# A fused mLSTM and sliding-window attention trunk: x loaded in one row, gate weights on ScalarE's DMA queue, the input gate scaled on ScalarE, two weight units multiplied by their gain beside the gate scans

## The chip, the core and the metric

The kernel runs on one core of a Trainium2 chip. Its time is device microseconds from launch to end. An engine is named here as in the trace: PE (matrix products), DVE (vector), ACT (scalar, table functions), POOL (GpSimd), SP (issues DMAs). SPq and ACTq are the DMA-issuing instructions on SP and on ACT; they run in the order of that engine's program.

## What is computed

One mLSTM layer with its SwiGLU, a shared K/V projection, one sliding-window attention layer with its SwiGLU, a final RMSNorm; x is 1024 x 1024, all in float32. The change lies in the first stage: the norm of x, the gates, and what the first head needs from them.

```python
def rmsnorm(x, g):
    return (x * lax.rsqrt(jnp.mean(x * x, axis=-1, keepdims=True) + EPS)) * g

def mlstm_mixer(x, w_in, b_gates, head_norm, w_out):      # x: rmsnorm of the input with a_norm
    proj = x @ w_in
    q, k, v, o, gates = jnp.split(proj, [QK_W, 2 * QK_W, 2 * QK_W + V_W, 2 * QK_W + 2 * V_W], axis=-1)
    gates = GATE_CAP * jnp.tanh((gates + b_gates) / GATE_CAP)      # GATE_CAP = 15
    ig, fg = jnp.split(gates, 2, axis=-1)                          # 4 heads each
    lf = jax.nn.log_sigmoid(fg)
    h = mlstm_chunkwise(q * DQK_A ** -0.5, k, v, ig, lf)           # running sums of lf, running maxima with ig
    h = h * lax.rsqrt(jnp.mean(h * h, axis=-1, keepdims=True) + EPS) * head_norm
    return (h.reshape(Bsz, S, V_W) * jax.nn.sigmoid(o)) @ w_out
```

## The kernel before

Every float32 product is made of three passes of split operands: a tile is copied rounded (`write_hi`, ACT) and the rest is subtracted (`write_lo`, mostly DVE). Weights of the first layer come in units of 128 columns: unit 0 holds the gate weights (`U_GATES`), units 1 to 6 the six column blocks of head 0 (`U_HEADS + 0` to `+ 5`). A unit is loaded into one of three `raw` buffers by SP, multiplied in place by the norm's gain on POOL (`gain`, L952), rounded into `w_split` by ACT (L1190) and subtracted by DVE (L1596; the unit `U_HEADS + 3` by POOL, L1094). Only then is its raw buffer free for the unit three later, for which SP waits.

The order is written out by hand, engine by engine; semaphores count the steps. The first stage is this.

- SP loads x in eight tiles of 128 rows (L647). After three of them it issues two loads of the gate weights (L658, L659: 1024 runs of 16 bytes each) and the gain (L650: 1024 runs of 4 bytes), then the other five tiles, then units 1 and 2.
- For each tile ACT squares and sums (L1195), DVE forms the mean (L1601), POOL takes the power -0.5 (L940), DVE scales the tile (`x_normed`, L1607), PE transposes it (L2137), ACT rounds the transpose (L1201) and DVE subtracts (L1614). POOL multiplies the gate unit by its gain between the fourth and the fifth power; ACT and DVE split the gate unit at tile 5.
- PE multiplies the gate unit with all of x in two halves (L2103, L2105), then units 1 and 2. Beside these two units runs the gate chain on ACT and DVE: tanh of both gates (L1401, L1403), the input gate times 15 on DVE (L1836), exp (L1408), 1 + exp (L1838), ln (L1410), a correction (L1841), exp (L1413), product (L1845), log forget (L1847), the two scans (L1850 a sum, L1852 a maximum), differences (L1855 to L1864) and three last exponentials (L1416, L1418, L1419).
- PE then waits for ACT's L1418 (`gate_act` at least 5) and transposes the stacked gate rows (L2333); next come the v products (L2320 to L2324) and at last the chunk products of head 0 (L2369 on). POOL stores two gate rows and loads them spread over the partitions (L1098, L1103), SP waits for the end of the gate chain before it loads the first rows of `w_out`.
- `gate_dve` counts the DVE steps of the gate chain, `gate_act` those of ACT. POOL multiplies units 4, 5 and 6 by the gain as they arrive, without looking at these counts.

Of the kernel before, what the change touches and what calls it, by code (L numbers as in the profile page):

```python
# [151 lines left out]
def yoco_kernel(nc, x, a_norm, a_w_in, a_b_gates, a_head_norm, a_w_out, kv_norm, w_kv, b_kv,  # L152
# [169 lines left out]
    with ExitStack() as ctx:  # L322
# [301 lines left out]
        def _(sp):  # L624
# [21 lines left out]
            def load_x(t):  # L646
                sp.dma_start(X[:, t, :], x2[t * P:(t + 1) * P, :]).then_inc(x_loaded[t], 16)  # L647

            def load_gains(i, g):
                sp.dma_start(gcol[:, i, :], g.rearrange("(k p) -> p k", p=P), allow_slow_non_contiguous=True  # L650
                             ).then_inc(a_gain_loaded if i == 0 else gains_loaded, 16)

            for t in range(3):
                load_x(t)
            sp.wait_ge(gate_w_cleared, 1)
            gates = raw[:, 0, :].rearrange("p (k n) -> p k n", k=KT)
            g0 = 2 * NH_A * DQK + 2 * D
            sp.dma_start(gates[:, :, 0:NH_A], win[:, :, g0:g0 + NH_A]).then_inc(gate_w_loaded, 16)  # L658
            sp.dma_start(gates[:, :, 32:32 + NH_A], win[:, :, g0 + NH_A:g0 + 2 * NH_A]).then_inc(gate_w_loaded, 16)  # L659
            load_gains(0, a_norm[0, :])  # L660
            for t in range(3, TT):
                load_x(t)
# [39 lines left out]
            sp.wait_ge(gate_dve, 12)  # L702
            sp.wait_ge(gate_act, 7)
# [213 lines left out]
        def _(pool):  # L917
# [169 lines left out]
            for j in range(3, 6):  # L1087
                gain(Unit(U_HEADS + j))
# [21 lines left out]
            pool.wait_ge(gate_dve, 10)  # L1110
# [3 lines left out]
            pool.wait_ge(gate_act, 7)  # L1114
# [64 lines left out]
        def _(act):  # L1179
# [201 lines left out]

            K = uses.stage(NORM)
            for t in range(TT + 2):
                if t < TT:
                    act.wait_ge(x_loaded[t], 16)
                    square(0, t)
                if t >= 2:
                    xt_hi(K, t - 2)
                if t == 5:
                    write_hi(Unit(U_GATES))  # L1390
                if t >= TT:
                    write_hi(Unit(U_HEADS + t - TT))
# [16 lines left out]
            act.wait_ge(gate_dve, 3)  # L1409
# [4 lines left out]
            write_hi(Unit(U_HEADS + 3))  # L1414
            act.wait_ge(gate_dve, 8)
            act.activation(G[32:32 + NH_A, :], mrow[:], ACT.Exp, scale=-1.0).then_inc(gate_act, 1)  # L1416
            act.wait_ge(gate_dve, 12)
# [170 lines left out]
        def _(dve):  # L1588
# [227 lines left out]
            for t in range(TT + 2):  # L1816
                if t < TT:
                    mean_square(0, t)
                if t >= 2:
                    xt_lo(0, K, t - 2)  # L1820
                if t < TT:
                    x_normed(0, t)
                if t == 5:
                    write_lo(Unit(U_GATES))
            for j in range(2):
# [8 lines left out]
            K = uses.stage(BANK_45)  # L1834
            dve.wait_ge(bank_free[5], K[5] + 1)
            dve.tensor_scalar(ig[:], ig[:], GATE_CAP, None, ALU.mult).then_inc(gate_dve, 1)  # L1836
# [3 lines left out]
            dve.wait_ge(gate_dve, 3)  # L1840
            dve.scalar_tensor_tensor(enf[:], one_enf[:], -1.0, enf[:], ALU.add, ALU.subtract  # L1841
                                     ).then_inc(gate_dve, 1)
            dve.wait_ge(gate_dve, 4)
            dve.wait_ge(gate_act, 3)
            dve.tensor_tensor(enf[:], enf[:], fg[:], ALU.mult).then_inc(gate_dve, 1)  # L1845
            dve.wait_ge(gate_dve, 5)
            dve.tensor_tensor(lf[:], enf[:], lnu[:], ALU.subtract).then_inc(gate_dve, 1)  # L1847
            dve.wait_ge(gate_dve, 6)
            dve.wait_ge(const_step, 11)
            dve.tensor_tensor_scan(brow[:], chunk_mask[:], lf[:], 0.0, ALU.mult, ALU.add  # L1850
                                   ).then_inc(gate_dve, 1)
            dve.tensor_tensor_scan(mrow[:], lf[:], ig[:], 0.0, ALU.add, ALU.max  # L1852
                                   ).then_inc(gate_dve, 1)
            dve.wait_ge(gate_dve, 8)
# [4 lines left out]
            dve.wait_ge(gate_dve, 11)  # L1859
# [229 lines left out]
        def _(pe):  # L2089
# [209 lines left out]
            def head(h, turn, first):  # L2299
# [227 lines left out]
```

## Time and profile before

| | us |
|---|---|
| three runs: median (lowest, highest) | 2083.46 (2080.19, 2085.99) |
| the profiled execution, its own time | 2087.04 |
| its span in the trace | 2085.4 |
| PE busy in the span | 2020.8 (97%) |
| DVE, ACT, POOL busy | 1352.5, 925.8, 1211.7 |

The profiled execution is 3.6 us above the median of the three runs, and its span is 1.6 us shorter than its own time. Busy time of PE is modelled from pipelined matmuls, so 97% says where its waits are few, not that it runs at its peak. The whole change lies before 60 us of the span; what it moves later is only what starts earlier or later by it.

### The profile page before, as it was taken

The page shows a single profiled execution, that of the slowest core. Times are in us where ns is not written, and L with a number is a line of the kernel's source. Part 1 is how long each engine was busy: PE and PEld are TensorE (multiplying, and loading weights), DVE is VectorE, ACT ScalarE, POOL GpSimd, SP SyncE. Part 2 cuts the span into 40 slices and gives each one's busy share as a digit, 9 for nine tenths or more (in the row PEclk, how much of TensorE's full clock was granted, in tenths as well). Part 3 has the DMA queues.
Part 4 walks back from the last instruction along what each step waited for, and adds up shares of the span by engine and source line. Part 5 has one row for each costly group of instructions (what it writes and reads, how often), then busy time and mean ns, then how long its engine had stood idle before and what let it go on. Part 6 is the DMA issues. An engine that isn't in the chain of part 4 may idle for free.

```text
span 2085.4 us, 29248 instructions
## 1 busy us (share of the span) xinstructions
PE 2020.8 (97%) x9992; PEld 1660.8 (80%) x9992; DVE 1352.5 (65%) x1929; ACT 925.8 (44%) x1951; POOL 1211.7 (58%) x1058
## 2 busy tenths in 40 slices
PE   7999999899999999999999999899999999999998
PEld 6888988678888888888878666578788888888886
DVE  7663642568777767554665677768776676645566
ACT  6444343255555545422344454536544554532233
POOL 5531521464889988655664111264888788756565
PEclk9999999999999999999999999999999999999999
DMA  5655535843777787695844100564567666687673
GB/s 153 200 203 180 176 141 201 292 139 119 229 256 246 239 265 244 238 390 177 268 138 81 31 21 21 202 212 122 184 231 250 224 234 230 213 329 286 216 266 114
DMA packets 295431, 415.03 MB, mean 199 GB/s; under 512 B 40040, under 2 KB 218232, under 8 KB 295296
## 3 DMA queue, kind: packets, MB, share of 16 engines
q1 hardware_dynamic: 260752, 307.87, 45.0%
q10 hardware_dynamic: 33120, 100.68, 13.4%
q0 software_dynamic: 1424, 4.77, 0.8%
q8 instruction: 74, 1.21, 0.2%
q14 instruction: 61, 0.50, 0.1%
HBM read 259.09 MB, written 154.17 MB: 198 GB/s over the span
## 4 chain that ended last, share of the span: by engine, by line
PE 84%; DVE 7%; issue 3%; DMA 2%; ACT 2%; POOL 2%; SPq 0%; ACTq 0%; DVEq 0%; POOLq 0%
PE ps L2200 21%; PE ps L2202 20%; PE ps L2201 20%; PE ps L2103 8%; PE ps L2105 4%; PE ps L2464 1%; PE ps L2323 1%; PE ps L2324 1%; PE ps L2320 1%; PE ps L2493 1%; DVE mats L1643 1%; DMA scratch_y<-y_head 1%; PE ps L2483 1%; DVE forms L1741 1%; PE ps L2255 1%
## 5 line engine op out<-in xcount | busy, mean ns | idle before, releaser
L2200 PE MATMUL ps<-forms,mats 128*128 128x512 f32 x2016 | 790.7, 392 | 22.9 <-DVE X L1666 11.8
L2202 PE MATMUL ps<-forms,mats 128*128 128x512 f32 x2016 | 786.6, 390 | 0.0
L2201 PE MATMUL ps<-forms,mats 128*128 128x512 f32 x2016 | 786.2, 390 | 0.0
L1000 POOL TENSOR_TENSOR mats<-sum_a,mats 128x256 fp32r<-128x256 f32 (+2 forms) x384 | 405.8, 1062 | 373.2 <-ACT mats L1234 372.1
L2200 PEld LDWEIGHTS ps<-forms,mats 128*128 128x128 f32 x2016 | 379.6, 188 | 111.0 <-issue 19.6
L2202 PEld LDWEIGHTS ps<-forms,mats 128*128 128x128 f32 x2016 | 379.4, 188 | 79.9
L2201 PEld LDWEIGHTS ps<-forms,mats 128*128 128x128 f32 x2016 | 379.7, 188 | 77.4
L1666 DVE TENSOR_TENSOR X<-ps,X 128x512 f32<-128x512 f32 x390 | 267.6, 690 | 204.3 <-PE ps L2202 202.2
L1234 ACT ACTIVATE mats<-sum_a 128x256 fp32r<-128x256 f32 (+2 forms) x392 | 201.1, 516 | 336.6 <-PE ps L2202 317.0
L1643 DVE TENSOR_TENSOR mats<-stream_raw,mats 128x256 fp32r<-128x256 f32 (+2 forms) x302 | 279.0, 925 | 43.8 <-ACT mats L1234 43.1
L1234 ACT ACTIVATE mats<-stream_raw 128x256 fp32r<-128x256 f32 (+2 forms) x302 | 156.5, 520 | 250.8 <-PE ps L2202 237.0
L1622 DVE TENSOR_TENSOR prep_forms<-prep_raw,prep_forms 128x512 fp32r<-128x512 f32 x115 | 155.5, 1352 | 66.6 <-ACT prep_forms L1213 65.7
L986 POOL TENSOR_TENSOR sum_a<-stream_raw 128x256 f32<-128x256 f32 (+2 forms) x96 | 108.9, 1134 | 144.1 <-DVE mats L1643 55.9
L2103 PE MATMUL ps<-xT_hi,w_split 128*128 128x512 f32 x416 | 174.6, 420 | 0.0
L2103 PE MATMUL ps<-xT_lo,w_split 128*128 128x512 f32 x416 | 162.6, 391 | 0.0
L2105 PE MATMUL ps<-xT_hi,w_split 128*128 128x512 f32 x416 | 130.3, 391 | 0.0
L987 POOL TENSOR_TENSOR sum_a<-stream_raw 128x256 f32<-128x256 f32 (+2 forms) x96 | 121.3, 1264 | 0.0
L991 POOL TENSOR_TENSOR sum_a<-sum_a,stream_raw 128x256 f32<-128x256 f32 (+2 forms) x96 | 115.0, 1198 | 0.0
L995 POOL TENSOR_TENSOR sum_a<-stream_raw,sum_a 128x256 f32<-128x256 f32 (+2 forms) x96 | 109.5, 1140 | 6.9
L2103 PEld LDWEIGHTS ps<-xT_hi,w_split 128*128 128x128 f32 x416 | 78.2, 188 | 28.7 <-issue 13.9
L952 POOL TENSOR_TENSOR raw<-raw,gain_cols 128x1024 f32<-128x1024 f32 x34 | 73.2, 2163 | 39.4 <-DMA raw<-in_a_w_in_dram 21.9
L2105 PEld LDWEIGHTS ps<-xT_hi,w_split 128*128 128x128 f32 x416 | 78.1, 188 | 17.0
(230 smaller groups left out, 2705.7 us busy)
## 6 DMA issues: line engine op xcount, KB each, us to landing
forms<-scratch_forms ACTq DMA_DIRECT2D x182, 512.0 KB, 5.2
scratch_forms<-prep_forms SPq DMA_DIRECT2D x161, 512.0 KB, 3.4
stream_raw<-in_w_gate_up_dram SPq DMA_DIRECT2D x88, 512.0 KB, 5.4
scratch_forms<-head_forms SPq DMA_DIRECT2D x49, 512.0 KB, 2.6
scratch_hidden<-hidden SPq DMA_DIRECT2D x84, 256.0 KB, 5.4
prep_raw<-in_w_down_dram SPq DMA_DIRECT2D x38, 512.0 KB, 5.7
stream_raw<-scratch_hidden SPq DMA_DIRECT2D x32, 512.0 KB, 4.4
forms<-scratch_forms SPq DMA_DIRECT2D x28, 512.0 KB, 8.0
```

Source lines behind the costliest of these rows:

```text
L987: pool.tensor_tensor(s[2], a11, a21, ALU.subtract)
L991: pool.tensor_tensor(s[1], s[0], a11, ALU.subtract).then_inc(ssum, 2)
L1000: pool.tensor_tensor(blocks(m[:, q, 1, :], it.width), stream_source(it, q), blocks(m[:, q, 0, :].bitcast(F32), it.width), ALU.subtract).th ...
L1234: act.activation(blocks(mats[w][:, q, 0, :], w), stream_source(it, q), ACT.Copy).then_inc(hi_s, 4 if it.plain and q == 3 else 1)
L1622: dve.tensor_tensor(dst[:, 1, :], split_source(prep_raw[j % 2], prep_t, q), dst[:, 0, :].bitcast(F32), ALU.subtract).then_inc(prep_lo, 1)
L1643: dve.tensor_tensor(blocks(m[:, q, 1, :], it.width), stream_source(it, q), blocks(m[:, q, 0, :].bitcast(F32), it.width), ALU.subtract).the ...
L1666: dve.tensor_tensor(xv, ps[:, s + BANK_OF[q], :], before, ALU.add).then_inc(d_add, 1)
L2103: ms_ = [mm(ps[:, b + half, :], ah, t[:, c[half]], start=start and t is bh, stop=False) for half in halves for t in (bh, bl)]
L2105: ms_ += [mm(ps[:, b + half, :], al, bh[:, c[half]], start=False, stop=stop) for half in halves]
L2200: mm(dst, ah, bh, start=OPENS[q] and k == 0, stop=False, skip_group_check=True)
L2201: mm(dst, ah, bl, start=False, stop=False, skip_group_check=True)
L2202: m = mm(dst, al, bh, start=False, stop=k == w - 1, skip_group_check=True)
```

## The change

SP issues the eight tiles of x without anything between. The three loads of gate weights and gain go to ACT's queue; they stand ahead of ACT's first activation. The gate unit is split at tile 4 instead of 5. The input gate is scaled on ACT, after the third exponential, and the DVE step is gone; `U_HEADS + 3` is rounded by ACT ahead of the ln instead of after the exponential. POOL multiplies unit `U_HEADS + 3` where it did, but `U_HEADS + 4` and `+ 5` only after `gate_dve` has reached 5, which is the end of log forget. The counts that others wait for are shifted to match.

```diff
-            for t in range(3):
-                load_x(t)
-            sp.wait_ge(gate_w_cleared, 1)
-            gates = raw[:, 0, :].rearrange("p (k n) -> p k n", k=KT)
-            g0 = 2 * NH_A * DQK + 2 * D
-            sp.dma_start(gates[:, :, 0:NH_A], win[:, :, g0:g0 + NH_A]).then_inc(gate_w_loaded, 16)
-            sp.dma_start(gates[:, :, 32:32 + NH_A], win[:, :, g0 + NH_A:g0 + 2 * NH_A]).then_inc(gate_w_loaded, 16)
-            load_gains(0, a_norm[0, :])
-            for t in range(3, TT):
+            for t in range(TT):
                 load_x(t)
...
-            sp.wait_ge(gate_dve, 12)
-            sp.wait_ge(gate_act, 7)
+            sp.wait_ge(gate_dve, 11)
+            sp.wait_ge(gate_act, 8)
             load_head_row(0)
...
-            for j in range(3, 6):
-                gain(Unit(U_HEADS + j))
+            gain(Unit(U_HEADS + 3))
...
-            pool.wait_ge(gate_dve, 10)
+            pool.wait_ge(gate_dve, 5)
+            for j in range(4, 6):
+                gain(Unit(U_HEADS + j))
+            pool.wait_ge(gate_dve, 9)
             pool.dma_start(scr_negm, negm[:]).then_inc(negm_stored, 16)
...
+            act.wait_ge(gate_w_cleared, 1)
+            gates = raw[:, 0, :].rearrange("p (k n) -> p k n", k=KT)
+            g0 = 2 * NH_A * DQK + 2 * D
+            act.dma_start(gates[:, :, 0:NH_A], win[:, :, g0:g0 + NH_A]).then_inc(gate_w_loaded, 16)
+            act.dma_start(gates[:, :, 32:32 + NH_A], win[:, :, g0 + NH_A:g0 + 2 * NH_A]).then_inc(gate_w_loaded, 16)
+            act.dma_start(gcol[:, 0, :], a_norm[0, :].rearrange("(k p) -> p k", p=P), allow_slow_non_contiguous=True
+                          ).then_inc(a_gain_loaded, 16)
             K = uses.stage(NORM)
...
-                if t == 5:
+                if t == 4:
                     write_hi(Unit(U_GATES))
...
             act.activation(enf[:], fg[:], ACT.Exp, scale=-GATE_CAP).then_inc(gate_act, 1)
-            act.wait_ge(gate_dve, 3)
+            write_hi(Unit(U_HEADS + 3))
+            act.wait_ge(gate_dve, 2)
             act.activation(lnu[:], one_enf[:], ACT.Ln).then_inc(gate_act, 1)
             act.wait_ge(gate_act, 2)
 
             act.activation(fg[:], lnu[:], ACT.Exp, scale=-1.0).then_inc(gate_act, 1)
-            write_hi(Unit(U_HEADS + 3))
-            act.wait_ge(gate_dve, 8)
+            act.activation(ig[:], ig[:], ACT.Copy, scale=GATE_CAP).then_inc(gate_act, 1)
+            act.wait_ge(gate_dve, 7)
...
-                if t == 5:
+                if t == 4:
                     write_lo(Unit(U_GATES))
...
-            K = uses.stage(BANK_45)
-            dve.wait_ge(bank_free[5], K[5] + 1)
-            dve.tensor_scalar(ig[:], ig[:], GATE_CAP, None, ALU.mult).then_inc(gate_dve, 1)
+            uses.stage(BANK_45)
...
+            dve.wait_ge(gate_act, 4)
             dve.tensor_tensor_scan(mrow[:], lf[:], ig[:], 0.0, ALU.add, ALU.max
                                    ).then_inc(gate_dve, 1)
...
-                    pe.wait_ge(gate_act, 5)
+                    pe.wait_ge(gate_act, 6)
```

ACT's program from its start, before: the table load and the first squares stand first.

```order
L1195 ACT_TABLE_LOAD
L1195 ACTIVATE squares,ssq<-X 128x1024 x3
L1201 ACTIVATE xT_hi<-ps 128x4x128 x2
L1195 ACTIVATE squares,ssq<-X 128x1024
L1201 ACTIVATE xT_hi<-ps 128x4x128 x2
```

And now, with three DMAs ahead of the table load.

```order
L1379 DMA raw<-in_a_w_in_dram 128x8x4
L1380 DMA raw<-in_a_w_in_dram 128x8x4
L1381 DMA gain_cols<-in_a_norm_dram 128x8x1
L1189 ACT_TABLE_LOAD
L1189 ACTIVATE squares,ssq<-X 128x1024 x3
```

What moved: nothing in ACT's program can start before the three issues are through.

ACT's program in the gate chain, before (`w_split<-raw` is a `write_hi`).

```order
L1408 ACTIVATE exp_neg_f<-gate_f 4x1024
L1410 ACT_TABLE_LOAD
L1410 ACTIVATE ln_one_plus<-one_plus_exp 4x1024
L1413 ACT_TABLE_LOAD
L1413 ACTIVATE gate_f<-ln_one_plus 4x1024
L1190 ACTIVATE w_split<-raw 128x1024
L1416 ACTIVATE gate_stack<-m_row 4x1024
```

And now.

```order
L1409 ACTIVATE exp_neg_f<-gate_f 4x1024
L1184 ACTIVATE w_split<-raw 128x1024
L1412 ACT_TABLE_LOAD
L1412 ACTIVATE ln_one_plus<-one_plus_exp 4x1024
L1415 ACT_TABLE_LOAD
L1415 ACTIVATE gate_f<-ln_one_plus 4x1024
L1416 ACTIVATE gate_i<-gate_i 4x1024
L1418 ACTIVATE gate_stack<-m_row 4x1024
```

What moved: the rounding of unit 4 now stands ahead of the first table load of the chain, and the scaling of the input gate is new.

POOL's program between the norm and the first gate row that it stores, before (`raw<-raw,gain_cols` is a `gain`).

```order
L1085 MEMSET chunk_mask 4x8
L952 TENSOR_TENSOR raw<-raw,gain_cols 128x1024 x3
L1094 TENSOR_TENSOR w_split<-raw,w_split 128x1024
L1111 DMA scratch_neg_m<-neg_M 4x1024
L1098 DMA SwT<-scratch_neg_m 128x1024
```

And now.

```order
L1077 MEMSET chunk_mask 4x8
L944 TENSOR_TENSOR raw<-raw,gain_cols 128x1024
L1085 TENSOR_TENSOR w_split<-raw,w_split 128x1024
L944 TENSOR_TENSOR raw<-raw,gain_cols 128x1024 x2
L1105 DMA scratch_neg_m<-neg_M 4x1024
L1089 DMA SwT<-scratch_neg_m 128x1024
```

What moved: two of the three multiplications stand behind the subtraction of unit 4, and the diff makes them wait for log forget.

## Rows read from the trace of the kernel before

**Rows 1.** The page's head.
```profile
span 2085.4 us, 29248 instructions
```
**Rows 2.** Timeline, PE: start, length, instruction, idle time before it and its releaser.
```profile
15.62 3.89 PE L2137 MATMUL ps<-ident,x_normed 128*128 128x128 f32 x16 [3.06 <-DVE x_normed L1607]
...
21.28 0.57 PE L2103 MATMUL ps<-xT_hi,w_split 128*128 128x512 f32 x1
...
58.85 1.84 PE L2333 MATMUL ps<-ident,gate_stack 128*128 128x128 f32 x8 [2.66 <-ACT gate_stack L1418]
...
90.82 0.67 PE L2369 MATMUL ps<-v_one,SwT 128*128 128x257 f32 x2 [2.24 <-ACT v_one L1455]
```
**Rows 3.** The chain that ended last, in order of time: start, length, what.
```profile
60.78 5.47 DMA scratch_decay<-m_prev
...
86.95 2.60 DMA scratch_forms<-head_forms
```
**Rows 4.** Timeline, SP's DMA issues: start, time to issue.
```profile
2.32 0.43 SPq L658 DMA_DIRECT2D raw<-in_a_w_in_dram  x1
2.80 0.90 SPq L659 DMA_DIRECT2D raw<-in_a_w_in_dram  x1
3.74 3.40 SPq L650 DMA_DIRECT2D gain_cols<-in_a_norm_dram  x1
7.18 2.68 SPq L647 DMA_DIRECT2D X<-in_x_dram  x5
```
**Rows 5.** DMA issues by line: count, KB each, median us from issue to landing.
```profile
raw<-in_a_w_in_dram SPq DMA_DIRECT2D x2, 16.0 KB, 5.5
```
**Rows 6.** Stretches: length, PE busy (instructions), granted clock, DMA share, GB/s.
```profile
5.00:6.00 1.00, 0.00 (x0) 1.00 1.00 397
...
8.00:9.00 1.00, 1.00 (x7) 1.00 1.08 53
...
17.00:18.00 1.00, 1.00 (x5) 0.50 1.20 290
...
60.00:64.00 4.00, 4.00 (x27) 0.69 0.94 300
```
**Rows 7.** Timeline, ACT, the first stage.
```profile
0.94 1.28 ACT L1195 ACT_TABLE_LOAD   x1 [0.94 <-PEq L2516]
4.54 1.06 ACT L1195 ACTIVATE squares<-X 128x1024 f32<-128x1024 f32 x1 [2.32 <-DMA X<-in_x_dram]
...
11.18 1.06 ACT L1195 ACTIVATE squares<-X 128x1024 f32<-128x1024 f32 x1 [1.16 <-DMA X<-in_x_dram]
```
**Rows 8.** Timeline, DVE, the gate chain.
```profile
35.87 1.99 DVE L1836 TENSOR_SCALAR gate_i<-gate_i 4x1024 f32<-4x1024 f32 x1 [0.31 <-ACT gate_f L1403]
37.79 2.38 DVE L1838 TENSOR_SCALAR one_plus_exp<-exp_neg_f 4x1024 f32<-4x1024 f32 x1
40.20 2.80 DVE L1841 SCALAR_TENSOR_TENSOR exp_neg_f<-one_plus_exp,exp_neg_f 4x1024 f32<-4x1024 f32 x1
43.74 1.21 DVE L1845 TENSOR_TENSOR exp_neg_f<-exp_neg_f,gate_f 4x1024 f32<-4x1024 f32 x1 [0.74 <-ACT gate_f L1413]
44.99 3.30 DVE L1847 TENSOR_TENSOR log_forget<-exp_neg_f,ln_one_plus 4x1024 f32<-4x1024 f32 x1
48.33 2.28 DVE L1850 TENSOR_TENSOR_SCAN b_row<-chunk_mask,log_forget 4x1024 f32<-4x1024 f32 x1
```
**Rows 9.** Timeline, POOL.
```profile
0.93 0.95 POOL L918 MEMSET raw<- 128x1024 f32 x1 [0.29 <-POOLq L2516]
...
13.12 1.89 POOL L952 TENSOR_TENSOR raw<-raw,gain_cols 128x1024 f32<-128x1024 f32 x1
...
34.44 5.18 POOL L952 TENSOR_TENSOR raw<-raw,gain_cols 128x1024 f32<-128x1024 f32 x2 [3.02 <-DMA raw<-in_a_w_in_dram]
39.90 2.03 POOL L952 TENSOR_TENSOR raw<-raw,gain_cols 128x1024 f32<-128x1024 f32 x1 [0.27 <-DMA raw<-in_a_w_in_dram]
44.67 2.55 POOL L1094 TENSOR_TENSOR w_split<-raw,w_split 128x1024 fp32r<-128x1024 f32 x1 [2.73 <-ACT w_split L1190]
```

More of the change, by code:

```diff
@@ L650, in load_gains @@
                 sp.dma_start(gcol[:, i, :], g.rearrange("(k p) -> p k", p=P), allow_slow_non_contiguous=True
-                             ).then_inc(a_gain_loaded if i == 0 else gains_loaded, 16)
-            for t in range(3):
-                load_x(t)
-            sp.wait_ge(gate_w_cleared, 1)
-            gates = raw[:, 0, :].rearrange("p (k n) -> p k n", k=KT)
-            g0 = 2 * NH_A * DQK + 2 * D
-            sp.dma_start(gates[:, :, 0:NH_A], win[:, :, g0:g0 + NH_A]).then_inc(gate_w_loaded, 16)
-            sp.dma_start(gates[:, :, 32:32 + NH_A], win[:, :, g0 + NH_A:g0 + 2 * NH_A]).then_inc(gate_w_loaded, 16)
-            load_gains(0, a_norm[0, :])
-            for t in range(3, TT):
+                             ).then_inc(gains_loaded, 16)
+            for t in range(TT):
                 load_x(t)
@@ L1113, in _ @@
             load_neg_row(0)
-            pool.wait_ge(gate_act, 7)
+            pool.wait_ge(gate_act, 8)
             pool.dma_start(scr_einter, einter[:]).then_inc(rows_stored, 16)
@@ L1413, in _ @@
             act.activation(fg[:], lnu[:], ACT.Exp, scale=-1.0).then_inc(gate_act, 1)
-            write_hi(Unit(U_HEADS + 3))
-            act.wait_ge(gate_dve, 8)
+            act.activation(ig[:], ig[:], ACT.Copy, scale=GATE_CAP).then_inc(gate_act, 1)
+            act.wait_ge(gate_dve, 7)
             act.activation(G[32:32 + NH_A, :], mrow[:], ACT.Exp, scale=-1.0).then_inc(gate_act, 1)
-            act.wait_ge(gate_dve, 12)
+            act.wait_ge(gate_dve, 11)
             act.activation(G[64:64 + NH_A, :], brow[:], ACT.Exp).then_inc(gate_act, 1)
@@ L1833, in _ @@
             write_lo(Unit(U_HEADS + 2))
-            K = uses.stage(BANK_45)
-            dve.wait_ge(bank_free[5], K[5] + 1)
-            dve.tensor_scalar(ig[:], ig[:], GATE_CAP, None, ALU.mult).then_inc(gate_dve, 1)
+            uses.stage(BANK_45)
             dve.wait_ge(gate_act, 1)
             dve.tensor_scalar(one_enf[:], enf[:], 1.0, None, ALU.add).then_inc(gate_dve, 1)
-            dve.wait_ge(gate_dve, 3)
+            dve.wait_ge(gate_dve, 2)
             dve.scalar_tensor_tensor(enf[:], one_enf[:], -1.0, enf[:], ALU.add, ALU.subtract
                                      ).then_inc(gate_dve, 1)
-            dve.wait_ge(gate_dve, 4)
+            dve.wait_ge(gate_dve, 3)
             dve.wait_ge(gate_act, 3)
             dve.tensor_tensor(enf[:], enf[:], fg[:], ALU.mult).then_inc(gate_dve, 1)
+            dve.wait_ge(gate_dve, 4)
+            dve.tensor_tensor(lf[:], enf[:], lnu[:], ALU.subtract).then_inc(gate_dve, 1)
             dve.wait_ge(gate_dve, 5)
-            dve.tensor_tensor(lf[:], enf[:], lnu[:], ALU.subtract).then_inc(gate_dve, 1)
-            dve.wait_ge(gate_dve, 6)
             dve.wait_ge(const_step, 11)
@@ L1851, in _ @@
                                    ).then_inc(gate_dve, 1)
+            dve.wait_ge(gate_act, 4)
             dve.tensor_tensor_scan(mrow[:], lf[:], ig[:], 0.0, ALU.add, ALU.max
                                    ).then_inc(gate_dve, 1)
-            dve.wait_ge(gate_dve, 8)
+            dve.wait_ge(gate_dve, 7)
             dve.tensor_tensor(G[0:NH_A, :], ig[:], brow[:], ALU.subtract).then_inc(gate_dve, 1)
@@ L1858, in _ @@
             dve.tensor_copy(mprev[:, 0, 1:TT], chunks(mrow)[:, 0:TT - 1, P - 1]).then_inc(gate_dve, 1)
-            dve.wait_ge(gate_dve, 11)
+            dve.wait_ge(gate_dve, 10)
             last_negm = chunks(negm)[:, :, P - 1:P]
```

## The prediction, made before the changed kernel ran

> **What bounds the kernel now.** I read the page's head first, then PE's waits, then the chain of waits, since only a stretch in which PE waits, or runs at the lower clock, can give time back. The span is 2085.4 us [rows 1]; the change touches its first 60. PE waits there three times for something the change moves [rows 2]: 3.06 us before the transposes at 15.62, after which the granted clock stands at 0.50, the lower of its two levels (1.2 GHz) [rows 6]; 2.66 us at 58.85, for ACT's exponential of the gate rows, after which the clock means 0.69 over 60 to 64; and 2.24 us at 90.82, before the first chunk product. Between them PE runs without a gap, from the first gate product at 21.28 to 56.19 (58.85 less 2.66).
>
> The chain that ended last does not leave the gate work at 58.85 [rows 3]: it goes from the last exponentials over POOL's stored gate rows (the transfer of 5.47 us from 60.78), the sums and forms of the first `w_out` rows, to a store at 86.95 and so to 90.82. So what decides until 90.82 is the gate chain, not PE: a gate chain that ends d earlier brings the end forward by d, until PE itself is late. PE has 2.66 us of wait and about 1.3 us of slow clock to give at 58.85 ((1 - 0.69) x 4 us), and 2.24 us at 90.82, some 6 us together. A later gate chain is paid in full.
>
> So two sums are wanted: when the gate products of PE end (A), and how long the gate chain lasts from there (B).
>
> **A. The loads and the norm.** Before, the five last tiles of x are issued from 7.18 on, because three small transfers stand ahead; the third alone takes 3.40 us to issue [rows 4]. Their 3072 short runs also cost the DMA engines time: 53 GB/s from 8 to 9 us at a share of 1.08, where whole tiles give 397 [rows 6]. With x in one row, a tile takes 0.512 MB / 397 GB/s = 1.3 us, and tile 3 lands near 9 us instead of 11.18. ACT was done with the tiles before it at 10.02 (11.18 less its wait of 1.16 [rows 7]), so tile 3 starts 1.2 us earlier at best. From there ACT, DVE and PE are near their own pace (about 2 us a tile on ACT), and PE's transposes and the gain multiplication (1.89 us on POOL [rows 9], which holds DVE back) take part of it again. Splitting the gate unit at tile 4 puts its 1.06 us on ACT and 1.2 us on DVE before tile 5 instead of behind it: it makes the weights ready sooner, but the gate products wait for the transposes of tile 5, which come later by it. Following each engine's order, I get the gate products 0.7 us earlier. If the clock keeps its upper level (2.4 GHz), eight transposes take about 1.0 instead of 1.95 us (3.89 for sixteen [rows 2]), and the gain is 2.5 at most.
>
> Against it stands ACT's queue. Its three issues start at 1.9 us, when POOL has cleared the buffer [rows 9], and hold the table load (1.28 us [rows 7]) and the first square. With 0.43, 0.90 and again 0.43 us [rows 4] ACT is free at 1.9 + 1.76 + 1.28 = 4.9, 0.4 us behind the 4.54 of before, and that is absorbed where tile 2 is waited for. With 3.40 for the third it is 7.9, and A loses about 2 us instead of winning 0.7. I take the short issues: ACT's queue is empty at that moment, while SP's held three tiles.
>
> The larger unknown is when the small transfers land beside x. Alone behind three tiles the weights landed 5.5 us after issue [rows 5]. POOL takes up the gate unit after the fourth power, near 12 us, and the fifth power is queued behind it; DVE's fifth scaling, PE's fifth transposes and ACT's rounding wait for that. Landing by 12 costs nothing. If each DMA engine takes one run from either queue in turn, its 192 short runs go with 64 rows of 4 KB of x (0.16 us each: 10.5 us in all), and the rest beside the 512-byte runs of units 1 and 2; the gain then lands near 19 or 20 us. The gate multiplication moves from 13.12 to about 20 and A loses 7. The bounds of A are +2.5 and -8; I take +0.7.
>
> On how two queues share an engine the profile says nothing for such small runs. The Trainium skill (DMA: Bandwidth & Descriptors, section Queues, rings and completion order) has each engine go round the queues by packets of typically 9 to 17 descriptors; by that 192 short ones would be gone after 12 to 20 turns, and A stays at its small gain. No row here shows it.
>
> **B. The gate chain.** From both tanh at 35.87 to PE's transposes at 58.85 it lasts 23 us. Its DVE steps are stretched wherever POOL works. The 1 + exp from 37.79 ends at 40.17, 0.55 us after POOL's pair of multiplications ends at 39.62; the correction from 40.20 ends at 43.00, 1.07 after POOL's next ends at 41.93; log forget from 44.99 ends at 48.29, 1.07 after POOL's subtraction ends at 47.22 [rows 8, 9]. The product at 43.74, with POOL idle, takes 1.21. So DVE stands still until POOL is through.
>
> Now, on the old clock: exp ends at 36.93 (1.06 us, as any ACT pass over 1024 elements [rows 7]); 1 + exp no longer stands behind the input gate's 1.99 us, only behind the gain of unit 4, which ends near 37.0, and is done near 37.75; the correction is done near 39.0. ACT rounds unit 4 until 38.0, loads its table until 39.3, ln until 40.35, table until 41.65, exp until 42.7: 0.9 us before the old chain, whose product, waiting for it, started at 43.74 and so now starts at 42.8. Here the moved rounding is on the path, because the table load used to run while ln waited; it costs its 1.05 us and ln still starts 0.9 earlier. POOL's subtraction of unit 4 now lies beside the correction and ends near 41, so log forget takes 1.21 like the product and ends at 45.25 instead of 48.29. Gain so far: 3.0 us. The input gate on ACT (1.06 us until 43.8) is hidden: the second scan wants it at 47.5 (45.25 + 2.28).
>
> Then two multiplications come due at the very moment the first scan starts. No row of before has a scan beside POOL, so their price lies between 0 and 2 x 1.89 = 3.8 us. The nearest rows are the correction and log forget, which like the scan read two operands and were held to the full; I take 3.8. B then is 3.0 - 3.8 = 0.8 us longer. POOL has nothing else to do before it stores the first gate row, which comes after both scans, so POOL's own delay is free.
>
> The Trainium skill (SBUF, State Buffer, section Who interferes with whom) says that a vector instruction with two inputs in SBUF and a GpSimd instruction that reads SBUF exclude each other for their whole length. The rows of the correction and of log forget agree to a tenth of a us; by this rule moving work beside the scans only moves the stall, by the opposite assumption B gains all 3.0.
>
> **The sum.** A gives 0.7, B takes 0.8: +0.1 us on the profiled 2087.04 us, whose span is 2085.4. The profiled execution is 3.6 us above the median of 2083.46, so the forecast against that median is 2083.5.
>
> **The rivals.**
> 1. The scans are not held. B gains 3.0 and A 0.7: 2083.5 - 3.7 = 2079.8. For it: a scan takes 2.28 us for 1024 elements where the product takes 1.21, so it reads at about half the rate and may leave room. Against it: all three stretched steps above. If PE then waits over 3 us at 90.82, its clock can drop as it did after 3.06 and 2.66 us; up to 1.3 of the gain goes again.
> 2. The gate weights land late (slower). In turn with x, as worked out: A loses 7 and B 0.8, so 2083.5 + 7.8 = 2091.3. It decides from a landing after about 12 us and is paid one for one. For it: the short runs filled the DMA engines (share 1.08 at 53 GB/s) even alone. Against it: 4 us head start over the place where they are needed.
> 3. ACT is held at its third issue for the 3.40 us that SP was: A loses 2, B 0.8: 2086.3. For it: the same transfer behind the same two. Against it: no tiles of x in that queue.
>
> **Chances.** Forecast 0.37, rival 1 0.23, rival 2 0.25, rival 3 0.15. A change below 0.3% (6.2 us) is about what a measurement can't tell from none. The largest gain, 2.5 + 3.0, stays under it; only with an error of the runs does it pass: faster 0.08. Slower by more needs rival 2 with held scans: 0.19. The same 0.73. The forecast's own range is 2081 to 2086; with the rivals 2078 to 2091.5.
>
> **What will show it.** Squares of tile 3 start near 10 us; first square near 4.9 (7.9 under rival 3); the gate unit's multiplication near 12 (near 20 under rival 2); first gate product near 20.6; log forget takes 1.2 us; the scans and the step behind them together last 3.8 us longer than 2 x 2.28 + 1.21, or each its old length under rival 1; PE's wait at the gate transposes grows by 0.8 or vanishes, and in that case the wait before the first chunk product grows. I am wrong if the time falls by more than 6 us, or if a later stage, in which no instruction is changed, has its own new wait.

## The result: 12 us slower, outside the forecast range

| | before | after |
|---|---|---|
| median | 2083.46 us (7 runs) | 2095.64 us (7 runs) |
| profiled execution | 2087.04 us | 2100.39 us |
| its span | 2085.4 us | 2098.8 us |

The ratio after to before is 1.0057, with a 95% interval of 1.0039 to 1.0074; it leaves out one disturbed run of after (2882 us), and without that run after lies between 2090.95 and 2100.39 us. The forecast was 2083.5 us and its range ended at 2091.5. The change costs 12.2 us by the medians and 13.4 by the spans of the two profiled executions.

### The profile page after: what moved, and what is told of

It reads as the page before. It is cut to its first block, busy times and chain, and to the rows that moved or that the text cites. A ratio compares the mean times of both kernels' runs of the same rounds, so it can differ in the third digit from the quotient of the medians.

```text
span 2098.8 us, 29249 instructions
## 1 busy us (share of the span) xinstructions
PE 2024.4 (96%) x9992; PEld 1663.8 (79%) x9992; DVE 1348.7 (64%) x1928; ACT 926.8 (44%) x1952; POOL 1215.2 (58%) x1058
## 3 DMA queue, kind: packets, MB, share of 16 engines
q10 hardware_dynamic: 36240, 100.71, 13.4%
q8 instruction: 74, 1.21, 0.2%
## 4 chain that ended last, share of the span: by engine, by line
PE 84%; DVE 7%; issue 3%; ACT 2%; DMA 2%; POOL 2%; ACTq 1%; SPq 0%; POOLq 0%; DVEq 0%
PE ps L2201 20%; PE ps L2202 20%; PE ps L2203 20%; PE ps L2104 8%; PE ps L2106 4%; PE ps L2465 1%; PE ps L2324 1%; PE ps L2325 1%; PE ps L2321 1%; PE ps L2494 1%; DMA scratch_y<-y_head 1%; DVE mats L1645 1%; PE ps L2484 1%; DVE forms L1743 1%; PE ps L2370 1%
## 5 line engine op out<-in xcount | busy, mean ns | idle before, releaser
L2104 PEld LDWEIGHTS ps<-xT_hi,w_split 128*128 128x128 f32 x416 | 78.9, 190 | 29.0 <-issue 13.9
L2106 PEld LDWEIGHTS ps<-xT_hi,w_split 128*128 128x128 f32 x416 | 78.6, 189 | 17.3
```

The lines of the kernel that those rows point to most:

```text
L2104: ms_ = [mm(ps[:, b + half, :], ah, t[:, c[half]], start=start and t is bh, stop=False) for half in halves for t in (bh, bl)]
L2106: ms_ += [mm(ps[:, b + half, :], al, bh[:, c[half]], start=False, stop=stop) for half in halves]
```

## The profile after

The first view is the timeline of ACT from the start: start, length, instruction. A line on ACTq is the time that ACT spends issuing a transfer.

```profile
1.91 0.45 ACTq L1379 DMA_DIRECT2D raw<-in_a_w_in_dram  x1
2.40 0.60 ACTq L1380 DMA_DIRECT2D raw<-in_a_w_in_dram  x1
3.02 8.30 ACTq L1381 DMA_DIRECT2D gain_cols<-in_a_norm_dram  x1
11.35 1.28 ACT L1189 ACT_TABLE_LOAD   x1 [11.35 <-issue]
12.64 1.06 ACT L1189 ACTIVATE squares<-X 128x1024 f32<-128x1024 f32 x1
```

Against [rows 4, 7]: the first two issues are as short as SP's were, the third takes 8.30 us instead of 3.40, and the table load and the first square stand behind it. The first square moves from 4.54 to 12.64, by 8.1 us.

SP's own issues, in the same columns: all tiles of x leave in one row, as planned. Of the 6.06 us of the two unit loads behind them the second alone takes 5.57, so SP is held too, with no small transfer in its queue.

```profile
0.94 3.90 SPq L647 DMA_DIRECT2D X<-in_x_dram  x8
4.88 6.06 SPq L632 DMA_DIRECT2D raw<-in_a_w_in_dram  x2
```

The page's rows on DMA issues (count, KB each, median us from issue to landing) answer to [rows 5]:

```profile
raw<-in_a_w_in_dram ACTq DMA_DIRECT2D x2, 16.0 KB, 13.9
gain_cols<-in_a_norm_dram ACTq DMA_DIRECT2D x1, 4.0 KB, 16.3
```

13.9 instead of 5.5 us for the weights. The gain, issued at 3.02, lands at 19.3. Now POOL's timeline:

```profile
19.65 0.55 POOL L932 TENSOR_TENSOR rstd<-ms,neghalf 128x1 f32<-128x1 f32 x1 [2.07 <-DVE ms L1603]
20.18 1.89 POOL L944 TENSOR_TENSOR raw<-raw,gain_cols 128x1024 f32<-128x1024 f32 x1
...
53.84 7.77 POOL L944 TENSOR_TENSOR raw<-raw,gain_cols 128x1024 f32<-128x1024 f32 x2 [4.12 <-DVE log_forget L1847]
```

The gate unit's multiplication is at 20.18 instead of 13.12 [rows 9], as late as rival 2 had it. But its row has no wait: it follows the fourth power at once, which is itself late because ACT began late. By then the gain had landed. Two delays of about the same size lie over each other here, and a wait list names neither landing.

DVE's timeline in the gate chain, to be held against [rows 8]:

```profile
45.53 0.68 DVE L1838 TENSOR_SCALAR one_plus_exp<-exp_neg_f 4x1024 f32<-4x1024 f32 x1 [2.29 <-ACT exp_neg_f L1409]
46.25 1.21 DVE L1841 SCALAR_TENSOR_TENSOR exp_neg_f<-one_plus_exp,exp_neg_f 4x1024 f32<-4x1024 f32 x1
51.30 1.22 DVE L1845 TENSOR_TENSOR exp_neg_f<-exp_neg_f,gate_f 4x1024 f32<-4x1024 f32 x1 [3.84 <-ACT gate_f L1415]
52.55 1.22 DVE L1847 TENSOR_TENSOR log_forget<-exp_neg_f,ln_one_plus 4x1024 f32<-4x1024 f32 x1
53.80 2.28 DVE L1850 TENSOR_TENSOR_SCAN b_row<-chunk_mask,log_forget 4x1024 f32<-4x1024 f32 x1
56.01 3.91 DVE L1853 TENSOR_TENSOR_SCAN m_row<-log_forget,gate_i 4x1024 f32<-4x1024 f32 x1
59.95 2.74 DVE L1856 TENSOR_TENSOR gate_stack<-gate_i,b_row 4x1024 f32<-4x1024 f32 x1
62.62 1.21 DVE L1857 TENSOR_TENSOR neg_M<-b_row,m_row 4x1024 f32<-4x1024 f32 x1
```

Log forget takes 1.22 instead of 3.30. POOL's pair started at 53.84, with the first scan, and took 7.77 us for the work of 3.8. The first scan kept its 2.28; the second took 3.91 and the step behind it 2.74.

PE's timeline, for [rows 2]:

```profile
15.55 3.65 PE L2138 MATMUL ps<-ident,x_normed 128*128 128x128 f32 x16 [15.55 <-DVE x_normed L1609]
...
27.64 1.97 PE L2138 MATMUL ps<-ident,x_normed 128*128 128x128 f32 x8 [1.08 <-DVE x_normed L1609]
29.26 0.78 PE L2104 MATMUL ps<-xT_hi,w_split 128*128 128x512 f32 x1
...
67.52 1.09 PE L2334 MATMUL ps<-ident,gate_stack 128*128 128x128 f32 x8 [2.76 <-ACT gate_stack L1420]
...
100.04 1.20 PE L2370 MATMUL ps<-v_one,SwT 128*128 128x257 f32 x2 [2.71 <-ACT v_one L1457]
...
106.59 0.60 PE L2370 MATMUL ps<-v_one,SwT 128*128 128x257 f32 x2
```

The first transposes come at 15.55 and the first gate product 8.0 us later than before (29.26 against 21.28), the gate transposes 8.7, the first chunk product 9.2. The idle time before the last two is nearly that of before (2.76 and 2.71 against 2.66 and 2.24). What follows the second one is not. Two stretches of after (length, busy us of PE, PEld, DVE, ACT and POOL with their instructions, granted clock, DMA share, GB/s):

```profile
24.00:28.00 4.00, 2.33 (x10) 1.93 (x11) 4.00 (x8) 4.00 (x9) 0.82 (x2) 0.52 0.29 60
...
100.00:110.00 10.00, 9.96 (x32) 8.05 (x33) 3.04 (x10) 3.33 (x8) 2.25 (x2) 0.70 0.76 247
```

and the stretch of before in which the same chunk products lie:

```profile
90.00:100.00 10.00, 9.18 (x41) 7.79 (x42) 4.98 (x13) 4.09 (x10) 2.19 (x2) 1.00 0.82 278
```

In the first of them, before the first gate product, the clock stood at its lower level, as it did in before at 17 to 18 us [rows 6]; that loss is old. The second is new. After the wait of 2.71 us the granted clock means 0.70 over 10 us, after the wait of 2.24 it stayed at 1.00: 3.0 us ((1 - 0.70) x 10). The rows agree: from the first to the second chunk product it is 6.55 us in after (106.59 - 100.04), and was 3.70 before. The first head transposes come at 144.45 instead of 132.34, 12.1 late. The rest of the 13.4 is run-to-run: executions of every kernel here, before included (2078.8 to 2094.1 over the comparisons), differ by more than that, and the last section places a part of it.

So, by landmarks: 8.1 at ACT's third issue, 0.1 in the gate chain, 1.0 in the steps around these (9.2 at the first chunk product), 2.9 of lower clock behind the chunk wait, 1.3 spread over the 1950 us that follow.

## The experiments

Theory 1: the loads cost it all, through ACT's held issue. Rivals: through the late landing; through the chain. The table holds landmarks of each profiled execution (start times, us; "head transposes" are the first ones of head 0, L2295 in before) and the medians; the kernels of one group ran on one chip with their own runs of before. "Chain" is from the exponential of the forget gate (ACT; before, DVE's step at 35.87, which starts with it) to the gate transposes.

| kernel | first square | first gate product | gate transposes | chain | chunk product | head transposes | median | ratio to before, interval |
|---|---|---|---|---|---|---|---|---|
| before | 4.54 | 21.28 | 58.85 | 23.0 | 90.82 | 132.34 | 2082.8 to 2086.5 |  |
| after | 12.64 | 29.26 | 67.52 | 23.1 | 100.04 | 144.45 | 2095.64 | 1.0057, 1.0039 to 1.0074 |
| loads back | 4.51 | 21.40 | 59.22 | 23.4 | 91.36 | 132.88 | 2086.32 | 1.0013, 1.0001 to 1.0025 |
| loads only | 12.70 | 28.18 | 65.97 | 22.1 | 98.03 | 141.15 | 2090.70 | 1.0037, 1.0022 to 1.0053 |
| gain first | 5.94 | 26.59 | 64.85 | 23.1 | 96.58 | 139.74 | 2088.54 (one run) |  |
| gain on SP | 5.66 | 25.18 | 64.53 | 23.1 | 96.40 | 139.55 | 2095.00 | 1.0049, 1.0031 to 1.0067 |
| gains off the scans | 4.65 | 22.11 | 58.73 | 20.2 | 90.70 | 133.85 | 2084.76 | 0.9992, 0.9975 to 1.0009 |
| gains at arrival | 4.66 | 22.29 | 58.77 | 21.2 | 90.75 | 132.26 | 2087.85 | 1.0009, 0.9994 to 1.0025 |
| x waits | 8.75 | 25.37 | 64.85 | 23.1 | 96.67 | 139.79 | 2095.78 (one run) |  |
| five tiles | 4.52 | 21.66 | 57.65 | 20.2 | 89.54 | 132.69 | 2084.15 | 0.9994, 0.9978 to 1.0009 |
| chain only | 4.54 | 20.77 | 56.11 | 20.3 | 88.09 | 129.61 | 2080.76 | 0.998, 0.9964 to 0.9996 |
| chain, five tiles | 4.38 | 20.32 | 55.83 | 20.4 | 87.97 | 131.09 | 2081.34 | 0.9968, 0.9953 to 0.9984 |

**Loads back.** After, with the loads of before:

```diff
-            for t in range(TT):
+            for t in range(3):
+                load_x(t)
...
+            load_gains(0, a_norm[0, :])
+            for t in range(3, TT):
                 load_x(t)
...
-            act.dma_start(gates[:, :, 0:NH_A], win[:, :, g0:g0 + NH_A]).then_inc(gate_w_loaded, 16)
...
```

> The changed kernel with its loads as before: the three small transfers back on SP behind three tiles of x; the gate chain stays changed. Theory H (ACT is held 8.3 us at its third DMA issue, and that is the loss): the first square is back at 4.5 us, the gate chain lasts its 23.1 us, and the time is that of before within 1.5 us, 2082 to 2085. Theory S (the multiplications beside the scans are the loss): it stays at 2090 or above.

Measured 1.0013: most of the loss is gone, and the landmarks return to those of before within 0.6 us. The median, 2086.32, is 1.3 us above the expected 2085. The scans are held as in after, so the stall has nothing to do with the loads. PE's wait at the gate transposes was 3.12 us.

**Loads only.** Before, with only the loads' part of the change (the same lines, the other way round).

> The kernel before with nothing changed but the loads: x in one row on SP, the three small transfers on ACT's queue. Theory H: ACT's third issue takes about 8.3 us, the first square starts near 12.6, and the time is 2091 to 2097. Theory S: at most 2086.

Measured 1.0037, 7.9 us by the medians (0.3 us under the expected range); with the 3.5 us of the kernel above that makes 11.4 of after's 12.2. By the intervals the two parts are 5 to 11 and 0 to 5 us, so the sum fits and is no sharp test. Its timeline of ACT repeats the held issue:

```profile
3.02 8.35 ACTq L1379 DMA_DIRECT2D gain_cols<-in_a_norm_dram  x1
```

The first gate product stands at 28.18, 1.1 us ahead of after's 29.26: here the gate unit is split at tile 5, there at tile 4, and its rounding then stands before tile 5's transposes (the idle 1.08 us at 27.64 in after).

**Gain first.** After, with the gain's transfer ahead of the weights. It doesn't wait for the cleared buffer and goes out at 0.94. Is it the third place that is slow, or the transfer of 4-byte runs?

```diff
+            act.dma_start(gcol[:, 0, :], a_norm[0, :].rearrange("(k p) -> p k", p=P), allow_slow_non_contiguous=True
+                          ).then_inc(a_gain_loaded, 16)
             act.wait_ge(gate_w_cleared, 1)
...
```

> The changed kernel with the gain's transfer first on ACT's queue and the two of gate weights behind it. If ACT is held at whatever comes third behind two transfers of 1024 short runs, the second weight transfer now takes about 8 us to issue and the first square stays near 12.6. If it is held by the gain's own 4-byte runs, the hold is at the first issue. If neither, the first square is near 5 us and the span falls by about 8.

Its timelines of ACT and, below it, of POOL:

```profile
0.94 0.47 ACTq L1376 DMA_DIRECT2D gain_cols<-in_a_norm_dram  x1
1.92 0.40 ACTq L1381 DMA_DIRECT2D raw<-in_a_w_in_dram  x1
2.35 2.27 ACTq L1382 DMA_DIRECT2D raw<-in_a_w_in_dram  x1
...
5.94 1.06 ACT L1189 ACTIVATE squares<-X 128x1024 f32<-128x1024 f32 x1
```

```profile
18.42 1.90 POOL L944 TENSOR_TENSOR raw<-raw,gain_cols 128x1024 f32<-128x1024 f32 x1 [4.92 <-DMA raw<-in_a_w_in_dram]
```

The third issue is again the held one, now a weight transfer, for 2.27 us: none of the three outcomes expected. So the kind of transfer isn't it, and the place alone isn't the price either: the first transfer had a head start and was landed at 6.2 (5.3 us after issue). In all kernels with three such transfers on ACT the hold ended 0.6 to 3.5 us before the first of them had landed (after 11.32 and 14.8; "loads only" 11.37 and 14.9; here 4.62 and 6.2; "x waits", below, 7.43 and 8.0). What the third waited for is seen in the DMA view, which counts what each queue has begun in a window (queue: packets, MB, share of the engines). ACT's queue, from 0 to the end of the hold, in after and then here:

```profile
q10 hardware_dynamic: 718, 0.01, 3.6%
```

```profile
q10 hardware_dynamic: 898, 0.00, 10.8%
```

Each short run is one packet, so of the 3072 runs sent 2354 and 2174 were still to go ("loads only": 2373). SP's queue shows the same. In after its second unit load was through at 10.94:

```profile
q1 hardware_dynamic: 886, 3.25, 80.0%
```

SP had sent 1024 rows of x and 2 x 1024 runs of units; 2186 were left. In "five tiles", below, the second gate transfer was held already, and at its end 451 of 2688 were gone, so 2237 left:

```profile
3.82 2.99 SPq L659 DMA_DIRECT2D raw<-in_a_w_in_dram  x1
```

```profile
q1 hardware_dynamic: 451, 1.66, 68.6%
```

ACT's first two transfers, 2048 runs, were never held. So neither the third place nor ACT is what counts: an issue is through only once some 2200 to 2400 runs or fewer are left in its queue. That figure is an estimate from these counts; no run set the amount by design, and where a queue drained fast (before, "x waits") fewer, about 1500, were left. And with the hold nearly gone, the landing comes out from under it: POOL waits 4.92 us for the weights, and the first gate product is still 5.3 us late.

**Gain on SP.** After, with the gain's transfer as SP's first:

```diff
+            sp.dma_start(gcol[:, 0, :], a_norm[0, :].rearrange("(k p) -> p k", p=P), allow_slow_non_contiguous=True
+                         ).then_inc(a_gain_loaded, 16)
             for t in range(TT):
                 load_x(t)
...
-            act.dma_start(gcol[:, 0, :], a_norm[0, :].rearrange("(k p) -> p k", p=P), allow_slow_non_contiguous=True
-                          ).then_inc(a_gain_loaded, 16)
```

> The changed kernel with the gain issued by SP ahead of x, so that ACT issues only two small transfers. Theory H alone: ACT is free near 3.0 us, the first square is near 4.7, the time falls to 2083 to 2085. Theory H with L (a small transfer that shares the DMA engines with x lands late): the gate weights still land near 15 and 17 us, so POOL multiplies them near 17.3 and not 13, the fifth power stands behind it, and the time stays 3 to 5 us above before: 2086 to 2089.

Timelines of ACT and of POOL:

```profile
3.06 1.28 ACT L1191 ACT_TABLE_LOAD   x1 [3.06 <-issue]
5.66 1.06 ACT L1191 ACTIVATE squares<-X 128x1024 f32<-128x1024 f32 x1 [1.32 <-DMA X<-in_x_dram]
```

```profile
17.01 1.90 POOL L946 TENSOR_TENSOR raw<-raw,gain_cols 128x1024 f32<-128x1024 f32 x1 [3.46 <-DMA raw<-in_a_w_in_dram]
```

ACT has sent its transfers by 3.06 and is ready at 4.3 (3.06 + 1.28), sooner than the 4.9 of the prediction; the first square then waits for x. The weights landed 7.9 and 14.5 us after issue (at 9.8 and 16.9), and POOL waits 3.46. The gate transposes are 5.7 us later than before's instead of 8.7. So the two causes aren't a sum: the late landing alone costs 5.7 to 6.0 us (this kernel, "gain first"), and taking away the hold on top of it returns 3. The hold without the landing, at its full length, was not run. In time this version is not told from after (1.0049 against 1.0057), and its median of 2095.00 lies above the expected 2086 to 2089. The traced execution, 2087.64, is the fastest of its six; it is one of three that lack a wait of 4 to 5 us near 410, told in the last section, so its landmarks stand for the first 140 us and not for the median.

**X waits.** After, with SP holding tiles 3 to 7 until the small transfers have landed:

```diff
             for t in range(TT):
+                if t == 3:
+                    sp.wait_ge(gate_w_loaded, 32)
+                    sp.wait_ge(a_gain_loaded, 16)
                 load_x(t)
```

> The changed kernel, but SP issues the tiles of x from the fourth on only once the gate weights and the gain have landed. If the small transfers are late because they share the DMA engines with the row of x (landing at 14.8, 17.3 and 19.3 us in the changed kernel), they now land within 6 us of their issue, near 7 to 9, and the third issue holds ACT for at most 4 us. If ACT's queue itself is slow with short runs, they still land after 14.

ACT's timeline, then the page's rows on DMA issues:

```profile
3.02 4.41 ACTq L1384 DMA_DIRECT2D gain_cols<-in_a_norm_dram  x1
7.46 1.28 ACT L1192 ACT_TABLE_LOAD   x1 [7.46 <-issue]
8.75 1.06 ACT L1192 ACTIVATE squares<-X 128x1024 f32<-128x1024 f32 x1
```

```profile
raw<-in_a_w_in_dram ACTq DMA_DIRECT2D x2, 16.0 KB, 6.1
gain_cols<-in_a_norm_dram ACTq DMA_DIRECT2D x1, 4.0 KB, 6.3
```

With only three tiles of x beside them the small transfers land in 6.1 us, nearly the 5.5 of [rows 5], and the hold is halved, 4.41 us. The same queue and order, only less of x: the row of x on SP makes both the landing and the hold long. What remains is not x's doing alone: ACT's queue begins its first run only at 5.7 us here (5.6 in after), 3.7 us after the issue. The kernel has a single run, so its time says little.

**Gains off the scans.** Loads back, and `U_HEADS + 4` and `+ 5` multiplied elsewhere, the first beside ACT's table load and exponential that follow the ln, the second after the first gate row is stored:

```diff
-            pool.wait_ge(gate_dve, 5)
-            for j in range(4, 6):
-                gain(Unit(U_HEADS + j))
+            pool.wait_ge(gate_dve, 3)
+            gain(Unit(U_HEADS + 4))
             pool.wait_ge(gate_dve, 9)
...
             load_neg_row(0)
+            gain(Unit(U_HEADS + 5))
```

> As e1_loads_back, but POOL multiplies unit U_HEADS + 4 from the DVE correction on (gate_dve at least 3, while DVE waits for ACT's table load and exponential) and unit U_HEADS + 5 only after the load of the first negative-maximum row. If the scans are held up by POOL (e1: second scan 3.91 instead of 2.25, the step behind it 2.74 instead of 1.21), both go back to their own length, the gate chain from exp to the gate transposes falls from 23.4 to about 20.3 us, PE no longer waits there, and the first chunk product comes about 3 us before e1's 91.4; time 2079 to 2082. If the gate chain is not what sets the end up to the first chunk product, the time does not move: 2083 to 2086.

DVE's timeline:

```profile
46.83 1.21 DVE L1848 TENSOR_TENSOR log_forget<-exp_neg_f,ln_one_plus 4x1024 f32<-4x1024 f32 x1
48.08 2.28 DVE L1851 TENSOR_TENSOR_SCAN b_row<-chunk_mask,log_forget 4x1024 f32<-4x1024 f32 x1
50.28 2.25 DVE L1854 TENSOR_TENSOR_SCAN m_row<-log_forget,gate_i 4x1024 f32<-4x1024 f32 x1
52.57 1.21 DVE L1857 TENSOR_TENSOR gate_stack<-gate_i,b_row 4x1024 f32<-4x1024 f32 x1
```

Against after: 2.25 for 3.91 and 1.21 for 2.74. That is 3.2 us of stall, and the chain is 20.2 instead of 23.1 to 23.4: the two multiplications cost what the rest of B gains. The time didn't follow (0.9992; 2079 to 2082 was expected). In the traced execution the gate products, at low clock this time (0.52, 0.50 and 0.70 over 16 to 20, 20 to 24 and 24 to 28 us), put the exponential at 38.57, 2.8 us later than in "loads back"; that it was so in the other executions is not shown.

**Gains at arrival.** Loads back, all three multiplications as early as before the change:

```diff
-            gain(Unit(U_HEADS + 3))
+            for j in range(3, 6):
+                gain(Unit(U_HEADS + j))
...
```

> As e1_loads_back, but POOL multiplies units U_HEADS + 4 and + 5 as they arrive, as the kernel before did; what is left of the change is the input gate on ACT and the rounding of U_HEADS + 3 moved ahead of the ln. The scans take 2.28 and 2.25 us again, 1 + exp, the correction or log forget are held instead by POOL. If the price is the overlap itself wherever it lies, the gate chain lasts 22 to 23.5 us and the time is that of e1 within 2 us; if only the scans are dear, it lasts about 20.5.

The chain is 21.2: without a multiplication beside the scans, but with the stretched 1 + exp and product (1.85 and 2.54 us). That is between the two lengths expected (22 to 23.5, about 20.5): an overlap costs there too, but less. 1.0009 cannot be told from no change.

**Five tiles.** "Gains off the scans", with the small transfers on SP behind five tiles of x instead of three.

```diff
-            for t in range(3):
+            for t in range(5):
```

> c1_gains_off_scans with the three small transfers on SP behind five tiles of x instead of three. Tile 3 then lands near 9 and its square starts near 10.1 instead of 11.15, the small transfers land near 12 to 13.5, just before POOL wants them. First gate product 0.5 to 1.5 us earlier than 21.3, time 0.5 to 1.5 us below c1. If they land after 14, the fifth power waits and the time is c1's or worse.

Against "gains off the scans" tile 3's square comes 0.9 us earlier, the first gate product 0.45 and the gate transposes 1.1; the time is not told from before's.

**Chain only.** Before, with the gate chain of "gains off the scans" and nothing else: loads and the gate unit's split at tile 5 are those of before.

```diff
-            for j in range(3, 6):
-                gain(Unit(U_HEADS + j))
+            gain(Unit(U_HEADS + 3))
...
+            act.activation(ig[:], ig[:], ACT.Copy, scale=GATE_CAP).then_inc(gate_act, 1)
...
-            dve.tensor_scalar(ig[:], ig[:], GATE_CAP, None, ALU.mult).then_inc(gate_dve, 1)
```

> The kernel before with the gate chain of c1_gains_off_scans and nothing else: loads as before, the gate unit split at tile 5. The gate chain from exp to the end of ACT's row exponential lasts 20.0 us (c1) instead of 22.9. If the 2 to 2.8 us that c1 lost in the gate products against e1 come from the split at tile 4 (a gap of about 1 us before the transposes of tile 5, and the lower clock after it), they are gone: exp starts near 35.9, the first chunk product near 88, time 2079 to 2082 and below c1. If that clock falls by the execution and not by the order, v2 is no better than c1: 2082 to 2085.

**Chain, five tiles.** The same with the small transfers behind five tiles.

> v2_chain_only with the three small transfers on SP behind five tiles of x. As v1 against c1: the square of tile 3 near 10.2 instead of 11.1, the first gate product about 0.5 us earlier, the time 0 to 1 us below v2. If the small transfers land after 13.7, POOL and the fifth power wait and it is above v2.

Both beat before, and so after: 0.998 (0.9964 to 0.9996) and 0.9968 (0.9953 to 0.9984), some 4 to 7 us, the first of them with an interval that ends just short of 1. Between the two nothing is resolved. "Chain only" also tests the path that the prediction had: with the exponential where it was (35.85 against 35.87) a chain shorter by 2.7 us brings the first chunk product forward by 2.7. At the head transposes the traces show a gain of 2.7 and 1.2 us only; the rest of what the times show has no place in them. PE's timeline of "chain only":

```profile
20.77 0.50 PE L2105 MATMUL ps<-xT_hi,w_split 128*128 128x512 f32 x1
```

With the split at tile 5 PE waits 0.41 us before tile 5's transposes, at tile 4 it waits 1.08 ("gains off the scans"). The granted clock over 20 to 24 us was 1.00 in both of these kernels and 0.81 in before, all split at tile 5, and 0.50 in "gains off the scans", "gains at arrival" and "five tiles". "Loads back", split at tile 4 too, had 1.00, so that the split lowers the clock is likely and not shown.

## Why the prediction was wrong

**The failed step is in A, the term for ACT's third issue:** "With 0.43, 0.90 and again 0.43 us [rows 4] ACT is free at 1.9 + 1.76 + 1.28 = 4.9", with its reason "ACT's queue is empty at that moment, while SP's held three tiles". The third issue measured 8.30 us, the first square 12.64. The reason was the error. An empty queue was no help: ACT's was empty and then filled by its own two transfers of 1024 runs, against which SP's three tiles of x (384 rows) are few. The third was through only when 2354 of 3072 runs were left (counted under "Gain first"), and the queue drained slowly because SP sent eight tiles of x at the same time (compare "X waits"). How slowly, the DMA view of after shows from 8 to 11 us, SP's queue and then ACT's:

```profile
q1 hardware_dynamic: 328, 1.19, 98.2%
q10 hardware_dynamic: 328, 0.01, 6.3%
```

One short run passes for each row of x. This is the very turn-taking that the prediction worked out for rival 2; it had not been asked what it does to an issue.

**Rival 3 named the mechanism and mis-sized it.** It carried the 3.40 us of [rows 4] over unchanged and so lost 2 us. But that row was taken while SP could not send x, since the hold was on SP itself: the very thing that the change moved away. The price of a stall had been read under the condition that the change removes. Measured 8.30, and A loses 8.0 us, the lower bound of the sum, which I had put on the landing.

**Rival 2 was right on its own fact and not on its path.** It was paid at a landing and needed one run in turn with a row of x; the gain was to land near 19 or 20 us and landed at 19.3, the gate unit's multiplication was to come near 20 and came at 20.18. But the landing held nobody in after, since ACT was later still; its price appears only when the hold is taken away (4.92 and 3.46 us of wait). The rule of the Trainium skill that was weighed (DMA: Bandwidth & Descriptors, Queues, rings and completion order) would, as the prediction read it, have had the short ones gone early; the weights landed at 14.8 and 17.3. That reading let several short runs pass for each row of x (and 192 by 9 are 22 turns, not 20). The trace shows 328 against 328 over 8 to 11 us, 554 against 551 over 11 to 14, and single runs in turn: 272 of the 328 are followed 6 ns later by the start of a packet of SP's queue. "Gain first" has 390 against 413 from 6.2 to 10 us, but at its opening, from 3.0 to 4.62, 898 against 83, which is why its first transfer was landed in 5.3 us where 64 turns of 0.16 us would be 10.2. Why the opening is not in turn stays open.

I treated rivals 2 and 3 as alternatives. They have one cause and were both true. Nothing in the sum had a case for both; and the range ended at 2091.5 though the sum's own bounds, 8 us for A and 0.8 for B, reach 2092.3. By the landmarks it was 9.2 us up to the chunk product and 2.9 of lower clock behind it (below), 2095.6 from 2083.46.

**B was right in its mechanism.** Gain without the scans 3.0 forecast, 2.8 measured (23.0 against 20.2, "gains off the scans"). Held scans 3.8 forecast, 3.2 measured. With equal loads B is 0.4 us longer ("loads back", 23.4, against before, 23.0) and 1.0 with the late ones (after, 23.1, against "loads only", 22.1); forecast 0.8. Rival 1 fell: the second scan takes 3.91 against 2.25. That the first was not held, and that the stall fell on the second and the step behind it, was not foreseen; POOL's first multiplication waited for the first scan instead (7.77 us for two).

**Not in the sum:** the clock after the chunk wait. The text said of the wait at 90.82 that a longer one could drop the clock, but only under rival 1. It grew by 0.5 us, to 2.71, and 2.9 us were lost to the lower clock behind it, in the traced execution.

**A's small gain** (0.7) never had its test in after. x in one row, or in five tiles, with the small ones behind it on SP, did bring tile 3 forward, and "five tiles" gains 1.1 us at the gate transposes; "chain, five tiles" 0.3.

## What to carry to other kernels

Before a price is read from a stall, ask what else was under way then, and whether the change leaves it so: the 3.40 us were true only while the large loads stood behind the stalled queue. Count the runs that a queue would hold: here an issue waited whenever more than some 2400 would have been left in it. Transfers of many short runs, put on a compute engine's queue, then hold that engine's first instructions, and beside large loads they drain at one run per large row; what wins here is to leave them in the queue that only loads, and to place POOL's two-operand work where DVE waits for ACT. When two delays have one cause, price them together: removing the hold alone returned 3 of 8.7 us.

## What the hardware showed beside this

- The first two transfers of 1024 short runs issue in 0.40 to 0.60 us on ACT, the third in 2.27 to 8.35, depending on how fast the queue drains. The same holds for 1024 runs of 512 bytes on SP: 0.45 us for the first unit in after, 5.57 for the second.
- DVE's scan with two operands and a POOL multiplication exclude each other as the other two-operand steps do: 3.91 us against 2.25. The Trainium skill (SBUF, State Buffer, Who interferes with whom) states it for two-input instructions in general; here it holds for scans. They take turns by whole instructions: the scan that had just started kept its 2.28 us, and POOL waited.
- A wait of 2.71 us of PE before the first chunk product was followed by a granted clock of 0.70 over 10 us in after, one of 2.24 in before was not. In "chain only" and "gains at arrival" waits of 2.73 and 2.70 us at the same place were followed by 1.00, in seven kernels waits of 2.06 to 2.71 by 0.83 or 0.84, in "loads back" one of 2.48 by 1.00. So the length of the wait alone does not decide it, and the 0.70 of after is the deepest of twelve.
- Part of the spread between executions has a place. In after PE waits near 421 us for DVE, far behind anything that the change moves (PE's timeline):

```profile
421.39 0.77 PE L2201 MATMUL ps<-forms,mats 128*128 128x512 f32 x1 [4.96 <-DVE X L1668]
```

Nine of the twelve profiled executions have it (before: 4.68 us at 409.04); those of "gain first", "gain on SP" and "chain only" don't. From the first product of the `forms` at 365.86 in before to the next norm's transposes at 429.15 it is 63.0 to 65.5 us in the nine and 56.2 to 57.9 in the three: about 7 us, more than most differences in the table. What decides it is open. For this reason the medians and their intervals carry the verdicts above, and the landmarks of one execution only the places.
